# Four-layer hybrid decoder trunk in float32 on one core: a ninth chunk of the FFN's down projection in seven products, and tile 0's norm behind an FFN from three sums

## The reference

```python
def rmsnorm(x, g):
    return x * lax.rsqrt(jnp.mean(x * x, axis=-1, keepdims=True) + EPS) * g

def swiglu(x, wg, wu, wd):                    # wg, wu: 1024 x 2816, wd: 2816 x 1024
    return (jax.nn.silu(x @ wg) * (x @ wu)) @ wd

for i in range(4):
    x = x + 0.5 * rmsnorm(swiglu(rmsnorm(x, g[0]), ...), g[1])
    x = x + rmsnorm(mixer(rmsnorm(x, g[2])), g[3])
    x = x + 0.5 * rmsnorm(swiglu(rmsnorm(x, g[4]), ...), g[5])
```

## Time and profile before

| | |
|---|---|
| median of 3 runs | 1990.48 us (1990.48 to 1991.07) |
| the profiled execution's own time | 1992.52 us |
| its span in the profile | 1990.7 us |
| PE busy | 1980.4 us, 99% |
| PE weight loads busy | 1846.1 us, 93% |
| DVE busy | 1571.4 us, 79% |
| ACT busy | 1089.6 us, 55% |
| POOL busy | 26.5 us, 1% |
| moved by DMA | 386.37 MB, 194 GB/s |

### The profile page before, as it was taken

The page is one execution under the profiler, slowest core; times in us unless marked ns, Lnnn a source line. Parts: engine busy times, 40 slices in busy tenths (PEclk is TensorE's granted clock), DMA queues, the critical chain, the costliest instruction groups (busy, mean ns, idle before and its releaser), DMA issues.

```text
span 1990.7 us, 36138 instructions
## 1 busy us (share of the span) xinstructions
PE 1980.4 (99%) x14806; PEld 1846.1 (93%) x14806; DVE 1571.4 (79%) x1783; ACT 1089.6 (55%) x1208; POOL 26.5 (1%) x52
## 2 busy tenths in 40 slices
PE   9999999999999999999999999999999999999998
...
GB/s 261 232 211 188 252 167 195 190 213 189 202 213 178 218 185 150 164 134 190 203 195 214 191 191 216 235 142 148 212 190 211 192 199 203 232 192 159 211 190 106
DMA packets 56291, 386.37 MB, mean 194 GB/s; under 512 B 6752, under 2 KB 7136, under 8 KB 11232
## 3 DMA queue, kind: packets, MB, share of 16 engines
...
HBM read 383.39 MB, written 1.05 MB: 193 GB/s over the span
## 4 chain that ended last, share of the span: by engine, by line
PE 94%; DVE 3%; issue 1%; ACT 1%; DMA 1%; POOL 0%; DVEq 0%; POOLq 0%; ACTq 0%
PE ps L553 21%; PE ps L554 21%; PE ps L555 21%; PE ps L559 7%; PE ps L561 6%; PE ps L560 6%; PE ps L575 2%; PE ps L578 2%; PE ps L572 2%; PE ps L715 1%; PE ps L712 1%; PE ps L711 1%; DVE w_low L1615 1%; PE ps L594 1%; PE ps L923 0%
## 5 line engine op out<-in xcount | busy, mean ns | idle before, releaser
L1615 DVE TENSOR_TENSOR w_low<-raw,w_high 128x2048 fp32r<-128x2048 f32 x287 | 650.2, 2286 | 95.2 <-ACT w_high L1165 95.2
L553 PE MATMUL ps<-xT_both,w_high 128*128 128x256 f32 x2304 | 638.3, 277 | 0.7 <-DVE region L1673 0.7
L554 PE MATMUL ps<-xT_both,w_high 128*128 128x256 f32 x2304 | 637.0, 276 | 0.0
L555 PE MATMUL ps<-xT_both,w_low 128*128 128x256 f32 x2304 | 636.7, 276 | 0.0
L1165 ACT ACTIVATE w_high<-raw 128x2048 fp32r<-128x2048 f32 x287 | 545.9, 1910 | 43.1 <-DMA raw<-stream 33.5
L554 PEld LDWEIGHTS ps<-xT_both,w_high 128*128 128x128 f32 x2304 | 433.3, 188 | 0.0
L553 PEld LDWEIGHTS ps<-xT_both,w_high 128*128 128x128 f32 x2304 | 432.5, 188 | 0.9 <-issue 0.9
L555 PEld LDWEIGHTS ps<-xT_both,w_low 128*128 128x128 f32 x2304 | 432.6, 188 | 0.0
L1209 ACT ACTIVATE region<-ps 128x256 f32<-128x256 f32 x176 | 67.0, 381 | 434.3 <-PE ps L555 425.4
L559 PE MATMUL ps<-xT_both,w_high 128*128 128x256 f32 x736 | 207.7, 282 | 0.0
L560 PE MATMUL ps<-xT_both,w_low 128*128 128x256 f32 x736 | 205.1, 279 | 0.0
...
## 6 DMA issues: line engine op xcount, KB each, us to landing
...
```

The costliest lines, as they stand in the source:

```text
L553: nc.tensor.matmul(acc, lh, rh, start=start, stop=False, skip_group_check=goes_on)
L554: nc.tensor.matmul(acc, lh, rl, start=False, stop=False, skip_group_check=goes_on)
L555: return nc.tensor.matmul(acc, ll, rh, start=False, stop=stop, skip_group_check=goes_on)
L1615: nc.vector.tensor_tensor(w_low[:, p % RING, :], raw[:, p % RAW, :], w_high[:, p % RING, :], ALU.subtract).then_inc(piece_split, 1)
```

## The change

`SEVENS` becomes 9: chunk 8 of every FFN goes in seven products, and unit 8 takes in blocks 18 and 19. Behind it stand blocks 20 and 21 and two plain chunks, 9 and 10. The order of these is now: tile 0, chunk 9 left and right, chunk 10 left and right; tile 1, chunks 9 and 10 left, chunks 9 and 10 right. The next sublayer's piece 2 is split ahead of the joint (`FFN_PIECES + 2`), not in it. `join` keeps its first five additions; the two that finish tile 1's banks are `join_second`, around the split of block 21.

In the seven joints behind an FFN, tile 0 takes another chain (`short_chain`). With yg = y times gain and r = the post-norm factor, the mean square of the new x is mean(x²) + 2 r mean(x yg) + r² mean(yg²); mean(x²) is left from the joint before. ACT now squares y only after DVE has made yg (`square_y` waits for `y_gained`), then squares yg (`square_gained`); DVE makes the cross sum (`tensor_tensor_reduce`). The second power no longer waits for the new x. x and xn are written in halves of 512 columns, and PE transposes the halves apart: behind 3 of the last six matmuls the first half, two matmuls later the second. In the other joints `pre_norm` of tile 0 is written in halves too, of the same content.

```diff
...
-SEVENS = 8
+SEVENS = 9
...
-    return GU_BANK + (i % 2 if i < EARLY or i >= BLOCKS - 4 else 0)
+    return GU_BANK + (i % 2 if i < EARLY or i >= BLOCKS - 2 else 0)
...
-    return {4: 4, 5: 6}.get(i, i + i // 2 - 1) if i < BLOCKS - 2 else 3 * CHUNKS - 5 + i - (BLOCKS - 2)
+    return {4: 4, 5: 6}.get(i, i + i // 2 - 1)
...
-    return {0: 5, CHUNKS - 3: 3 * CHUNKS - 3, CHUNKS - 2: 3 * CHUNKS - 2, CHUNKS - 1: 3 * CHUNKS - 1}.get(c, 3 * c + 4)
+    return {0: 5, CHUNKS - 1: 3 * CHUNKS - 1}.get(c, 3 * c + 4)
...
+        def short_norm(joint, t):
+            return after_ffn(joint) and joint < SUBLAYERS and t == 0
...
-            def transpose_x(joint, t):
-                pe.wait_ge(xn_ready, TILES * joint + t + 1)
+            def transpose_x(joint, t, halves=(0, 1)):
                 if joint == 0 and t == 0:
                     pe.wait_ge(ident_landed, 16)
-                for b in range(2):
+                for b in halves:
+                    pe.wait_ge(xn_ready, 3 * joint + (3 if t else b + 1))
...
+                def chunk(c, t, half):
+                    p = w0 + down_piece(c)
+                    for j in range(FT):
+                        cols = slice(j * D + half * 512, j * D + half * 512 + 512)
+                        tok, at = slice(t * P, (t + 1) * P), h_slot(FT * c + j)
+                        ends = c == CHUNKS - 1 and j == FT - 1
+                        if ends and t == 1 and half == 1:
+                            transpose_next(sub, (0,))
+                            acc = ps[:, Y_BANK + 3, :]
+                            for rh in (w_high, w_low):
+                                nc.tensor.matmul(acc, oT_hi[:, at, tok], rh[:, p % RING, cols], start=False, stop=False,
+                                                 skip_group_check=True)
+                            transpose_next(sub, (1,))
+                            return nc.tensor.matmul(acc, oT_lo[:, at, tok], w_high[:, p % RING, cols], start=False, stop=True,
+                                                    skip_group_check=True)
+                        last = products(ps[:, Y_BANK + 2 * t + half, :], oT_hi[:, at, tok], oT_lo[:, at, tok],
+                                        w_high[:, p % RING, cols], w_low[:, p % RING, cols], False, ends, goes_on=True)
+                    return last
+                pe.wait_ge(joined, 7 * ffn_no(sub) + 5)
+                for c in range(CHUNKS - 2, CHUNKS):
+                    pe.wait_ge(hT_split, s0 + splits_up_to(FT * c + 1))
+                    weights_ready(w0 + down_piece(c))
                     for half in range(2):
...
+                        last = chunk(c, 0, half)
+                        if c == CHUNKS - 1:
+                            last.then_inc(y_ready, 1)
+                pe.wait_ge(joined, 7 * ffn_no(sub) + 7)
+                chunk(CHUNKS - 2, 1, 0)
+                chunk(CHUNKS - 1, 1, 0).then_inc(y_ready, 1)
+                chunk(CHUNKS - 2, 1, 1).then_inc(piece_used, 1)
+                chunk(CHUNKS - 1, 1, 1).then_inc(piece_used, 1)
...
+            def square_gained(joint, half):
+                cols = slice(half * 512, (half + 1) * 512)
+                act.wait_ge(y_gained, 2 * TILES * (joint - 1) + half + 1)
+                nc.scalar.activation(norm_scratch[:, D + half * 512:D + (half + 1) * 512], xn[:, 0, cols], ACT.Square, scale=1.0 / 32,
+                                     accum_out=mean_gained[:, half:half + 1]).then_inc(gained_mean, 1)
...
-                    square_y(joint, 0, 0)
-                    if after_ffn(joint):
-                        high(w0 + 2)
-                    square_y(joint, 0, 1)
+                    for half in range(2):
+                        square_y(joint, 0, half)
+                        if short_norm(joint, 0):
+                            square_gained(joint, half)
...
-                unit(SEVENS - 2)
-                silu_of(sub, BLOCKS - 6)
-                high(w0 + 27)
-                silu_of(sub, BLOCKS - 5)
-                chunk_high(sub, SEVENS)
-                high(w0 + 28)
-                first_part_out(sub)
-                high(w0 + 29)
                 silu_of(sub, BLOCKS - 4)
-                h_high(sub, BLOCKS - 4)
                 high(w0 + 30)
                 high(w0 + 31)
                 silu_of(sub, BLOCKS - 3)
-                h_high(sub, BLOCKS - 3)
                 high(w0 + 32)
+                first_part_out(sub)
+                chunk_high(sub, SEVENS)
+                high(w0 + FFN_PIECES)
+                high(w0 + FFN_PIECES + 1)
                 silu_of(sub, BLOCKS - 2)
                 h_high(sub, BLOCKS - 2)
-                high(w0 + FFN_PIECES)
+                high(w0 + FFN_PIECES + 2)
...
+            def short_chain(joint):
+                n, k = TILES * (joint - 1), ffn_no(joint - 1)
+                halves = [slice(half * 512, (half + 1) * 512) for half in range(2)]
+                dve.wait_ge(gain_landed, 16 * (1 + 2 * joint))
+                for half, cols in enumerate(halves):
+                    dve.wait_ge(y_ready, y_before(joint) + half + 1)
+                    nc.vector.tensor_tensor(xn[:, 0, cols], ps[:, Y_BANK + half, :], gain[:, 0, cols],
+                                            ALU.mult).then_inc(y_gained, 1)
+                    dve.wait_ge(y_gained, 2 * n + half + 1)
+                    nc.vector.tensor_tensor_reduce(norm_scratch[:, 2 * D + half * 512:2 * D + (half + 1) * 512], xn[:, 0, cols],
+                                                   x[:, 0, cols], 2.0 / D, 0.0, ALU.mult, ALU.add,
+                                                   cross[:, half:half + 1]).then_inc(cross_ready, 1)
+                    dve.wait_ge(y_mean, 2 * n + half + 1)
+                    if half == 0:
+                        nc.vector.tensor_scalar(mean_first[:, 0:1], mean_y[:, 0, 0:1], EPS / Y_SCALE[KINDS[joint - 1]] ** 2,
+                                                None, ALU.add).then_inc(y_eps, 1)
+                    else:
+                        dve.wait_ge(y_eps, n + 1)
+                        nc.vector.tensor_tensor(mean_eps[:, 0:1], mean_y[:, 0, 1:2], mean_first[:, 0:1],
+                                                ALU.add).then_inc(y_sum, 1)
+                dve.wait_ge(cross_ready, 2 * k + 2)
+                nc.vector.tensor_tensor(both[:, 0:1], cross[:, 0:1], cross[:, 1:2], ALU.add).then_inc(added_ready, 1)
+                dve.wait_ge(gained_mean, 2 * k + 2)
+                nc.vector.tensor_tensor(both[:, 1:2], mean_gained[:, 0:1], mean_gained[:, 1:2], ALU.add).then_inc(added_ready, 1)
+                dve.wait_ge(added_ready, 3 * k + 2)
+                dve.wait_ge(y_rstd, n + 1)
+                nc.vector.scalar_tensor_tensor(out=added[:, :], in0=both[:, 1:2], scalar=rstd_y[:, 0:1], in1=both[:, 0:1],
+                                               op0=ALU.mult, op1=ALU.add).then_inc(added_ready, 1)
+                dve.wait_ge(added_ready, 3 * k + 3)
+                nc.vector.scalar_tensor_tensor(out=mean_eps[:, TILES:TILES + 1], in0=added[:, :], scalar=rstd_y[:, 0:1],
+                                               in1=mean_eps[:, TILES:TILES + 1], op0=ALU.mult,
+                                               op1=ALU.add).then_inc(x_sum, 1)
+                for half, cols in enumerate(halves):
+                    done = nc.vector.scalar_tensor_tensor(out=x[:, 0, cols], in0=xn[:, 0, cols], scalar=rstd_y[:, 0:1],
+                                                          in1=x[:, 0, cols], op0=ALU.mult, op1=ALU.add)
+                    if half == 0:
+                        done.then_inc(half_updated, 1)
+                        dve.wait_ge(half_updated, k + 1)
+                        dve.wait_ge(x_rstd, TILES * joint + 1)
+                    else:
+                        done.then_inc(x_updated, 1)
+                        dve.wait_ge(x_updated, n + 1)
+                    nc.vector.scalar_tensor_tensor(out=xn[:, 0, cols], in0=x[:, 0, cols], scalar=rstd_x[:, 0:1],
+                                                   in1=gain[:, 1, cols], op0=ALU.mult, op1=ALU.mult).then_inc(xn_ready, 1)
...
+                for cols in (slice(0, D),) if t else (slice(0, D // 2), slice(D // 2, D)):
...
+                        nc.vector.scalar_tensor_tensor(out=xn[:, t, cols], in0=x[:, t, cols], scalar=rstd_x[:, t:t + 1],
+                                                       in1=gain[:, 1, cols], op0=ALU.mult, op1=ALU.mult).then_inc(xn_ready, 1)
...
+            def join_second(sub, half):
+                n = 7 * ffn_no(sub)
+                dve.wait_ge(joined, n + (1 if half == 0 else 2))
+                u = sums[:, 3 * half * HALF:(3 * half + 1) * HALF]
+                nc.vector.tensor_tensor(ps[:, 6 + half, :], ps[:, 6 + half, :], u, ALU.add).then_inc(joined, 1)
...
-                unit(SEVENS - 2)
-                times_up(sub, BLOCKS - 6)
-                low(w0 + 26)
-                low(w0 + 27)
-                times_up(sub, BLOCKS - 5)
```

(36 more changed lines are left out.)

82 lines of the change are left out of this document (35 added, 47 removed).

## The result

The changed kernel takes 1995.66 us, median of 12 runs (1993.02 to 1997.41), beside 1990.64 us (1989.99 to 1991.53, 12 runs) for the kernel before on the same chip. The ratio is 1.0024 with a 95% interval of 1.0017 to 1.0031: about 5.0 us slower. The forecast was 1988.3 us, in a range that ended at 1990.8. It missed by 7 us, on the wrong side. The profiled execution took 1996.28 us, 3.8 us more than that of the kernel before.

A forecast was written before the change was run, and what follows sets the result against it. PE's count of matmuls at its pace was taken to bound the kernel. Terms −5.45 − 2.1 − 0.3 + 5.6 gave −2.2 us, from 1990.48 to 1988.3 us, range 1985.2 to 1990.8.

The forecast's parts named there:

- What PE saves: In each of eight FFNs one chunk takes 21 matmuls instead of 24: 0.68 us each, 5.45 us in all.
- bound from a unit's rest: Lower estimate of PE's saving, from a unit's time less its two blocks: 0.62 us per FFN, 4.96 in all.
- DVE up to the last block: Before block 21's multiply DVE runs without pause from piece 32 on, with about 0.65 us to spare.
- when the norm can begin: At joints behind an FFN, the norm starts as piece 35 ends, 4.70 us after B, the end of block 21.
- The chain from g: From the norm's start g: POOL's second power 4.29 to 4.84 us, normed left half at 5.66, right at 7.11.
- What PE finds: PE waits 0.21 us for the normed left half and 0.60 for the right; 5.6 us over seven joints.
- What the old joint gives back: Losses at the low parts of x vanish: 2.1 us in four joints and 0.3 in three.
- The signs: Expected in the profile: 24 fewer 512-column matmuls, transposes waiting at seven joints, DVE about 48 us busier, clock 1.00.
- The rule on waits between chained operations: On DVE, the skill's rule has such waits free, giving 1986.6 us, chance 0.06; rows say 0.12 us each.
- The slower rival: Before block 21, a late weight transfer for piece 32 or 34 makes DVE fall behind: 1995.4 us, chance 0.08.

The follow-up runs named there:

- experiment 2: The changed kernel, with PE transposing a constant tile for tile 0's normed x at seven joints, waiting only for cross sums and squares; 1991.18 us, ratio 1.0001.
- experiments 3: The changed kernel, but DVE writes the new x only after POOL's second power has come; 1998.63 us, ratio 1.0038.
- 4: The changed kernel with the update of x's left half cut into four operations of 128 columns; 1996.67 us, ratio 1.0027.
- 6: The changed kernel with right transposes behind the next sublayer's first four matmuls and x's left-half update in two 256-column operations; 1992.34 us, ratio 1.0007.
- experiment 1: The changed kernel with tile 0's old norm in all joints, x and xn still written in halves; 1995.16 us, ratio 1.0025.

## Why the prediction was wrong

- *What PE saves* (−5.45 us): somewhat too large. No run has the ninth chunk without the end order, but experiment 2 gives 0.62 us for an FFN without the waits and the last FFN 0.60, so 4.9 us in eight. The prediction's own bound from a unit's rest, 4.96, was the better value.
- *DVE up to the last block, when the norm can begin*: right, B + 4.69 for B + 4.70.
- *The chain from g*: this is the step that failed, in one term. "POOL again 4.29 to 4.84" was 4.39 to 5.38, because the row for it stood beside an idle DVE and the new one stands beside the update of x, which experiments 3, 4 and 6 show to be the cause. The four half-width operations behind it took their predicted times, 2.20 us together.
- *What PE finds*: wants at 10.21 (measured 10.22). Waits 0.76 and 0.50 where 0.21 and 0.60 stood, and 0.09 for a second group of transposes, which had no term: 1.35 us a joint, 9.5 in seven, instead of 5.6. The lengthened power is 0.44 of the joint's 0.54 us too much, 3.1 us in seven.
- *What the old joint gives back* (−2.4): right. The waits on the low parts are gone: a quick convolution falls from 91.32 us in the kernel before to 90.80 with the norm alone, by the 0.52 of the prediction, and the norm alone, without any other part of the change, gained 2.3 us.
- *The pace of the convolutions* had no term: the second step that failed. About 1.45 us twice, 2.9 us in the profiled execution. It is read from traces only; that it costs the runs as much as the profiled executions is argued.
- The sum with measured terms is −4.9 − 2.4 + 9.5 + 2.9 = +5.1 us, beside +5.0 measured. That it closes so well is partly luck: the kernel before's two profiled spans are 1990.7 and 1988.0 us, the changed kernel's 1994.5 and 1995.8, and the profiled difference is anything from 3.8 to 7.8.
- *The signs.* DVE became 62.9 us busier, not about 48. Its chain started on time all the same.
- The rule on waits between chained operations: the rows were right to be preferred. At joint 3 of the changed kernel the normed right half starts 0.78 us after x's right half, for which it waits, and x's right half 0.67 us after the normed left one, for which it doesn't. The slower rival named a late weight; none was late. It came to nearly its time for another reason.

The step behind both errors was to take each duration as a property of an operation. The comparison was not drawn that experiment 1 shows: under this end order the new norm reaches its first power 1.2 us later than the old, so that the two parts of the change, of which each looked like a gain, spoil each other. The norm alone gains 2.3 us, since its cover is long; with nine chunks in seven products and this end order the cover is 9 matmuls shorter, and either norm is then too late.
